# Twelve expert products grouped by PSUM bank: six into one bank, then six into the other

## The chip, the cores and the metric

The kernel runs on one core of a Trainium2 chip. The metric is the device time of one execution in microseconds (us), start to end, on that core. A core has TensorE (PE in the profile, with its weight loads as PEld), VectorE (DVE), ScalarE (ACT), GpSimd (POOL) and SyncE (SP), which here issues most of the DMAs. PE writes its results into PSUM, which has eight banks of 512 float32 columns in each of 128 partitions. The other engines read them there.

## What is computed

The reference is one layer of a hybrid model for 1024 tokens of width 1024: a norm, one projection, four mixers (sparse attention, a gated recurrent mixer, banded attention, differential attention), a gated sum, an output projection, a second norm, a router, and 32 experts. Each token goes to two experts, and the results are summed with the router's weights. The part around the change is the expert block:

```python
def expert_block(args):
    xb, e = args
    return (jax.nn.silu(xb @ w1[e]) * (xb @ w3[e])) @ w2[e]
```

`xb` are the rows of an expert's tokens (width 1024), `w1[e]` and `w3[e]` are 1024 x 512, and `w2[e]` is 512 x 1024, all float32.

## The kernel before

The layer runs in stages: `project`, `attend`, `mix`, `route`, `experts`, `combine`. The change is in `experts` (from L2101). It treats the 32 experts in order, two for each turn `i` of a loop (`j` is 0 or 1), with 96 token rows each (`CAP` = 96). There is one copy of each buffer for `j` = 0 and one for `j` = 1. Work for experts with more than 96 tokens stands behind it in `overflow`, and the change does not touch that.

A float32 product is made of three float32r products: each operand is split into a high part (a rounded copy) and a low part (what is left), and hi x hi, hi x lo and lo x hi are summed in PSUM. ScalarE makes the high part of the weights (`high_a` for w1 and w3 at L2326, `high_b` for w2 at L2335) in a ring of four buffers, `w_hi`. VectorE makes the low part in place of the weights (`low_a` at L2413, `low_b` at L2420).

The weights come in blocks of 1 MB: w1 and w3 of an expert in four (`wa`, L219; `q` = 0 to 3), w2 in two (`wd`, L223; `q` = 0, 1). SyncE issues the load of a block for the expert two further on as soon as PE has used that block (`a_used`, `b_used`).

PE's order of work for one expert is in `body`: `up` for `q` = 0 and 1, eight transposes that turn the next expert's rows (L2140), `up` for `q` = 2 and 3, `down` of the expert before, and four transposes of the hidden rows (L2146).

- `up(i, j, q)` (product at L2255) covers two blocks of K, `k` = 2q and 2q + 1, with the index `c`. The stationary operand is the transposed token block `x[:, k, :]`, 128 partitions x 96 columns. The moving operand is `w[:, c, m, :]`, 512 columns: `m` = 0 is w1, into bank 4 (`UP`), and `m` = 1 is w3, into bank 5. There are 2 x 3 x 2 = 12 products a call, 48 an expert.
- `down` (product at L2271) does the same for w2: the stationary operand is `x[:, f, :]` of the hidden rows, 128 x 96, and `h` picks one half of the 1024 output columns, into bank 6 (`Y`) or 7. There are 12 products for each of two `q`, 24 an expert.

After `up`, ScalarE takes the sigmoid of bank 4 (L2367), and VectorE multiplies (L2406, L2408). After `down`, ScalarE copies banks 6 and 7 out (L2350), and its queue stores them (L2352).

Three other stages have products of the same kind (float32r, 512 moving columns), with 128 stationary columns. L922 in `project` makes 24 products into a bank before it goes to the next. L1588, in the output projection, also makes 24. L1639, in `mix`, makes six:

```python
                for h in range(2):
                    cols = slice(h * 512, (h + 1) * 512)
                    for k in range(2):
                        ...
                        for r, (w, x) in enumerate(((w_h, y_hi[n]), (w_h, y_lo[n]), (w_l, y_hi[n]))):
                            ins = nc.tensor.matmul(psum[:, 2 * (c % 4) + h, :], w[:, k, :], x[:, k, cols],
```

In these three, too, the stationary operand is a high block twice and a low block once for each k. L2076, in `route`, is a series of small products.

Of the kernel before, what the change touches and what calls it, by code (L numbers as in the profile page):

```python
# [2100 lines left out]
def experts(nc, a, s):  # L2101
# [6 lines left out]
    wa_lo, w_hi, xg, xg_in = s.wa_lo, s.w_ring, s.xg, s.xg_in  # L2108
    wb_lo = [[sb(f"wb_lo{j}_{q}", [P, 2, DM], 128 + 16 * j + 8 * q, F32R) for q in range(2)] for j in range(2)]
    xT_hi = [sb(f"xT_hi{i}", [P, KC, CAP], 72 + 3 * i, F32R) for i in range(2)]  # L2110
    xT_lo = [sb(f"xT_lo{i}", [P, KC, CAP], 80 + 3 * i, F32R) for i in range(2)]
    hT_hi, hT_lo = sb("hT_hi", [P, FT, CAP], 78, F32R), sb("hT_lo", [P, FT, CAP], 86, F32R)
# [17 lines left out]
    def hi_a(j, q):  # L2130

        return w_hi[(6 * j + q) % 4][:, :].rearrange("p (c m n) -> p c m n", c=2, m=2)

    def hi_b(j, q):

        return w_hi[(6 * (j + 1) + 4 + q) % 4][:, :].rearrange("p (f n) -> p f n", f=2)

    def x_transposes(j):
        for c in range(KC):
            ins = nc.tensor.transpose(psum[:, c // 4, (c % 4) * CAP:(c % 4 + 1) * CAP],  # L2140
                                      xg[j][:, c * P:(c + 1) * P], s.ident[0:CAP, 0:CAP])
        return ins

    def h_transposes():
        for f in range(FT):
            ins = nc.tensor.transpose(psum[:, 2, f * CAP:(f + 1) * CAP], hid[:, f * P:(f + 1) * P],  # L2146
                                      s.ident[0:CAP, 0:CAP])
        return ins
# [16 lines left out]
    def loop(eng, body):  # L2165

        for j in range(2):
            body(0, j, j == 0, False)
        with eng.Fori(1, NE // 2 - 1) as i:
            for j in range(2):  # L2170
                body(i, j, False, False)
        for j in range(2):
            body(NE // 2 - 1, j, False, j == 1)

    def overflow(eng, body):

        blocks = eng.value_load(s.ov_i[0:1, 1, 0:1], min_val=0, max_val=N_OV)
        with eng.If(blocks > 0):
            with eng.Fori(0, N_OV) as b:
                body(b)  # L2180
# [4 lines left out]
    with nc.Block() as block:  # L2185
        @block.sync
        def _(sp):
            def refill(i, j, up, down):

                if up:  # L2190
                    for q in range(4):
                        sp.wait_ge(a_used, i * 8 + (4 * j - 8 + q + 1))
                        s.load_a(sp, i * 2 + j, j, q)
                if down:
                    for q in range(2):
                        sp.wait_ge(b_used, i * 4 + (2 * j - 6 + q + 1))
                        s.load_b(sp, i * 2 + (j - 1), 1 - j, q)

            refill(1, 0, True, False)
            refill(1, 1, True, True)  # L2200
            with sp.Fori(2, NE // 2) as i:
                for j in range(2):
                    refill(i, j, True, True)
            refill(NE // 2, 0, False, True)
            sp.wait_ge(b_used, 2 * NE)

            def body(b):
                sp.wait_ge(ov["go"], b + 1)
                e = expert_of(sp, b)
                for q in range(4):  # L2210
                    s.load_a(sp, e, 0, q, ov["weights"])
                for q in range(2):
                    s.load_b(sp, e, 0, q, ov["weights"])
            overflow(sp, body)
# [31 lines left out]
        @block.tensor  # L2246
        def _(pe):
            def up(i, j, q):

                pe.wait_ge(a_low, i * 8 + (4 * j + q + 1))  # L2250
                for c in range(2):
                    k = 2 * q + c
                    for x, w in ((xT_hi[j], hi_a(j, q)), (xT_hi[j], wa_lo[j][q]), (xT_lo[j], hi_a(j, q))):
                        for m in range(2):
                            ins = nc.tensor.matmul(psum[0:CAP, UP + m, :], x[:, k, :], w[:, c, m, :],  # L2255
                                                   start=(k == 0 and x is xT_hi[j] and w is not wa_lo[j][q]),
                                                   stop=(k == KC - 1 and x is xT_lo[j]))
                ins.then_inc(a_used, 1)

            def down(i, j, first):  # L2260

                pe.wait_ge(hT_low, i * 2 + (j + 1))
                if not first:
                    pe.wait_ge(y_taken, i * 2 + j)
                for q in range(2):
                    pe.wait_ge(b_low, i * 4 + (2 * j + q + 1))
                    for c in range(2):
                        f = 2 * q + c
                        for x, w in ((hT_hi, hi_b(j, q)), (hT_hi, wb_lo[j][q]), (hT_lo, hi_b(j, q))):
                            for h in range(2):  # L2270
                                ins = nc.tensor.matmul(psum[0:CAP, Y + h, :], x[:, f, :],  # L2271
                                                       w[:, c, h * 512:(h + 1) * 512],
                                                       start=(f == 0 and x is hT_hi and w is not wb_lo[j][q]),
                                                       stop=(f == FT - 1 and x is hT_lo))
                    ins.then_inc(b_used, 1)

            def body(i, j, start, last):
                if start:
                    pe.wait_ge(xg_in[0], 16)
                    x_transposes(0).then_inc(xT_ready, 1)  # L2280
                pe.wait_ge(xT_low, i * 2 + (j + 1))
                up(i, j, 0)
                up(i, j, 1)
                if not last:
                    pe.wait_ge(xg_in[1 - j], i * 16 + (16 + 16 * j))
                    x_transposes(1 - j).then_inc(xT_ready, 1)
                up(i, j, 2)
                up(i, j, 3)
                if not start:
                    down(i if j else i - 1, 1 - j, isinstance(i, int) and i * 2 + j == 1)  # L2290
                pe.wait_ge(hid_ready, i * 2 + (j + 1))
                h_transposes().then_inc(hT_ready, 1)
            loop(pe, body)
            down(NE // 2 - 1, 1, False)
            pe.wait_ge(y_taken, NE)

            def body(b):
                pe.wait_ge(ov["rows"], b * 16 + 16)
                x_transposes(0).then_inc(ov["xT"], 1)
                pe.wait_ge(ov["xT_taken"], b + 1)  # L2300
                pe.wait_ge(ov["weights"], b * 96 + 96)
                for k in range(KC):
                    for m in range(2):
                        ins = nc.tensor.matmul(psum[0:CAP, UP + m, :], xT_ov[:, k, :], wa[0][k // 2][:, k % 2, m, :],
                                               start=(k == 0), stop=(k == KC - 1))
                ins.then_inc(ov["up"], 1)
                pe.wait_ge(ov["hid"], b + 1)
                h_transposes().then_inc(ov["hT"], 1)
                pe.wait_ge(ov["hT_taken"], b + 1)
                for f in range(FT):  # L2310
                    for h in range(2):
                        ins = nc.tensor.matmul(psum[0:CAP, Y + h, :], hT_ov[:, f, :],
                                               wb[0][f // 2][:, f % 2, h * 512:(h + 1) * 512],
                                               start=(f == 0), stop=(f == FT - 1))
                ins.then_inc(ov["y"], 1)
            overflow(pe, body)
# [270 lines left out]
```

## Time and profile before

| | |
|---|---|
| Time, median of 3 runs | 1860.6 us (1859.17 to 1860.83) |
| Span of the profiled execution, first to last instruction | 1856.9 us |
| What lies around the span, against the median | 3.7 us |
| Mean granted TensorE clock over the span | 0.967 |
| PE busy | 1738.5 us (94%) |
| VectorE busy | 1457.9 us (79%) |
| ScalarE busy | 941.4 us (51%) |
| Expert products (L2255 and L2271), first and last start | 1230.4 and 1806.9 us |

How to read it: busy time is the time in which an engine has an instruction under way, and PE's products overlap each other, so that a product's duration is longer than the distance to the next start. The granted clock is TensorE's clock as a share of its full 2.4 GHz.

### The profile page before, as it was taken

To read this page: it belongs to the slowest core of one execution; us is meant where nothing else is said; L and a number is where in the kernel's file an instruction comes from. 1 tells how busy PE (TensorE), PEld (TensorE's weight loads), DVE (VectorE), ACT (ScalarE), POOL (GpSimd) and SP (SyncE) were. 2 spreads that over 40 slices of the span, in tenths; PEclk is the share of its full clock that TensorE was granted. 3 is DMA by queue.
4 is the path that set the end of the run, shared out by engine and by line. 5 is a ranking of instruction groups with operands and counts; after the bars stand their busy time and mean duration, and the time that the engine had idled before them with its cause. 6 is when DMAs were issued, how large, how long until landed. Compare 5 with 4: busy or idle time off the path is not lost. (4 is left out here: it accounts for less than half of the span.)

```text
span 1856.9 us, 24076 instructions
## 1 busy us (share of the span) xinstructions
PE 1738.5 (94%) x8726; PEld 1315.4 (71%) x8726; DVE 1457.9 (79%) x2108; ACT 941.4 (51%) x1207; POOL 151.7 (8%) x129
## 2 busy tenths in 40 slices
PE   7999999999999999999999989859999999999980
PEld 7768877777777777777767767747777777777750
DVE  5587869989788878766629965679999999999956
ACT  6533121133434445545556520147777877878752
POOL 1100000000000000000000000002212122122003
PEclk9999999999999999999999989869999999999995
DMA  5202222112443322313206820299999999999937
GB/s 198 68 11 82 84 75 69 57 57 74 164 136 118 109 65 66 136 54 108 80 35 253 312 83 35 94 339 374 393 398 405 396 395 404 392 400 404 404 116 285
DMA packets 75920, 358.76 MB, mean 193 GB/s; under 512 B 8636, under 2 KB 11228, under 8 KB 49340
## 3 DMA queue, kind: packets, MB, share of 16 engines
q1 hardware_dynamic: 66364, 324.08, 46.6%
q0 software_dynamic: 5888, 20.97, 3.4%
q10 hardware_dynamic: 3584, 12.58, 1.7%
q8 instruction: 52, 0.85, 0.2%
q14 instruction: 32, 0.26, 0.0%
HBM read 301.63 MB, written 55.98 MB: 193 GB/s over the span
## 5 line engine op out<-in xcount | busy, mean ns | idle before, releaser
L2413 DVE TENSOR_TENSOR wa_lo<-wa,w_hi 128x2048 fp32r<-128x2048 f32 x127 | 287.6, 2286 | 15.5 <-ACT w_hi L2326 14.1
L2326 ACT ACTIVATE w_hi<-wa 128x2048 fp32r<-128x2048 f32 x127 | 242.8, 1915 | 63.0 <-PE psum L2271 36.4
L1470 PE MATMUL psum<-h_hi,w_hi 128*128 128x512 f32 x512 | 213.2, 416 | 4.0 <-DVE w_lo L153 2.1
L1470 PE MATMUL psum<-h_hi,w_lo 128*128 128x512 f32 x512 | 205.5, 401 | 0.0
L1470 PE MATMUL psum<-h_lo,w_hi 128*128 128x512 f32 x512 | 203.0, 396 | 0.0
L167 DVE MAX8 top<-sel 128x8 f32<-128x384 f32 (+5 forms) x192 | 171.3, 892 | 4.8
L2420 DVE TENSOR_TENSOR wb_lo<-wd,w_hi 128x2048 fp32r<-128x2048 f32 x64 | 143.9, 2288 | 34.7 <-ACT w_hi L2335 34.7
L165 DVE MATCH_REPLACE8 sel<-top,sel 128x384 f32<-128x384 f32 (+5 forms) x192 | 168.1, 875 | 0.0
L2255 PE MATMUL psum<-w_hi,xT_hi 128*96 128x512 f32 x512 | 164.8, 403 | 1.9 <-DVE xT_lo L2428 1.9
L2255 PE MATMUL psum<-w_hi,xT_lo 128*96 128x512 f32 x512 | 160.6, 394 | 0.0
L2255 PE MATMUL psum<-wa_lo,xT_hi 128*96 128x512 f32 x512 | 160.5, 395 | 0.0
L1470 PEld LDWEIGHTS psum<-h_hi,w_hi 128*128 128x128 f32 x512 | 96.9, 189 | 46.4 <-issue 18.9
L2335 ACT ACTIVATE w_hi<-wd 128x2048 fp32r<-128x2048 f32 x64 | 122.4, 1914 | 3.8 <-PE psum L2255 2.3
L1197 ACT ACTIVATE pt<-psum 128x512 f32<-128x512 f32 (+3 forms) x144 | 61.3, 471 | 118.9 <-PE psum L1490 118.7
L922 PE MATMUL psum<-h_hi,w_hi 128*128 128x512 f32 x288 | 117.5, 408 | 0.0
L1470 PEld LDWEIGHTS psum<-h_hi,w_lo 128*128 128x128 f32 x512 | 96.6, 189 | 25.5 <-issue 5.1
L922 PE MATMUL psum<-h_hi,w_lo 128*128 128x512 f32 x288 | 112.6, 391 | 0.0
L922 PE MATMUL psum<-h_lo,w_hi 128*128 128x512 f32 x288 | 112.3, 390 | 0.0
L1470 PEld LDWEIGHTS psum<-h_lo,w_hi 128*128 128x128 f32 x512 | 97.1, 190 | 19.6 <-issue 2.7
L2255 PEld LDWEIGHTS psum<-wa_lo,xT_hi 128*96 128x96 f32 x512 | 83.1, 162 | 36.1
L2255 PEld LDWEIGHTS psum<-w_hi,xT_lo 128*96 128x96 f32 x512 | 83.1, 162 | 35.9
L2255 PEld LDWEIGHTS psum<-w_hi,xT_hi 128*96 128x96 f32 x512 | 78.7, 164 | 29.6 <-DVE xT_lo L2428 2.2
(378 smaller groups left out, 3387.6 us busy)
## 6 DMA issues: line engine op xcount, KB each, us to landing
wa<-expert_up SPq DMA_DIRECT2D x128, 1024.0 KB, 11.0
wd<-expert_down SPq DMA_DIRECT2D x64, 1024.0 KB, 11.1
w<-w_gate SPq DMA_DIRECT2D x32, 512.0 KB, 4.1
gate_pre<-gate_out SPq DMA_DIRECT2D x64, 256.0 KB, 3.2
gate<-gate_pre SPq DMA_DIRECT2D x32, 512.0 KB, 6.1
ys<-yo ACTq DMA_DIRECT2D x32, 384.0 KB, 6.9
w<-w_T SPq DMA_DIRECT2D x18, 512.0 KB, 3.8
ys<-zeros SPq DMA_DIRECT2D x7, 1152.0 KB, 5.9
```

The source lines that it names most:

```text
L165: link(nc.vector.match_replace(sc, top8[:, :], sc, TAKEN))
L167: link(nc.vector.max(top8[:, :], sc))
L922: ins = nc.tensor.matmul(psum[:, bank + h, :], w[:, k, :], x[:, k, h * 512:(h + 1) * 512], start=(k == 0 and r == 0), stop=(k == KC - 1 an ...
L1197: nc.scalar.activation(dst, src, ACT.Copy).then_inc(pt_copied, 1)
L1470: ins = nc.tensor.matmul(psum[:, 7, :], w[:, k, :], x[:, k, half * 512:(half + 1) * 512], start=(n == 0), stop=(n == BURST - 1))
L2255: ins = nc.tensor.matmul(psum[0:CAP, UP + m, :], x[:, k, :], w[:, c, m, :], start=(k == 0 and x is xT_hi[j] and w is not wa_lo[j][q]), sto ...
L2326: nc.scalar.activation(hi_a(j, q).rearrange("p c m n -> p (c m n)"), wa[j][q][:, :, :, :].rearrange("p c m n -> p (c m n)"), ACT.Copy).the ...
L2335: nc.scalar.activation(hi_b(j, q).rearrange("p f n -> p (f n)"), wb[j][q][:, :, :].rearrange("p f n -> p (f n)"), ACT.Copy).then_inc(b_hig ...
L2413: nc.vector.tensor_tensor(wa_lo[j][q][:, :, :, :].rearrange("p c m n -> p (c m n)"), wa[j][q][:, :, :, :].rearrange("p c m n -> p (c m n)" ...
L2420: nc.vector.tensor_tensor(wb_lo[j][q][:, :, :].rearrange("p f n -> p (f n)"), wb[j][q][:, :, :].rearrange("p f n -> p (f n)"), hi_b(j, q). ...
```

## The change

In `up`, the loop over `m` (the bank) moves from inside to outside. Before, each product goes to the other bank than the one before it; after, the six products of both `c` and the three terms go to bank 4, then the same six to bank 5. In `down`, the loop over `h` moves in the same way, inside each `q`. Waits, semaphore counts and operands are the same, and the last product of each twelve is the same one.

```diff
@@ up
-                for c in range(2):
-                    k = 2 * q + c
-                    for x, w in ((xT_hi[j], hi_a(j, q)), (xT_hi[j], wa_lo[j][q]), (xT_lo[j], hi_a(j, q))):
-                        for m in range(2):
+                for m in range(2):
+                    for c in range(2):
+                        k = 2 * q + c
+                        for x, w in ((xT_hi[j], hi_a(j, q)), (xT_hi[j], wa_lo[j][q]), (xT_lo[j], hi_a(j, q))):
                             ins = nc.tensor.matmul(psum[0:CAP, UP + m, :], x[:, k, :], w[:, c, m, :],
                                                    start=(k == 0 and x is xT_hi[j] and w is not wa_lo[j][q]),
                                                    stop=(k == KC - 1 and x is xT_lo[j]))
@@ down
-                    for c in range(2):
-                        f = 2 * q + c
-                        for x, w in ((hT_hi, hi_b(j, q)), (hT_hi, wb_lo[j][q]), (hT_lo, hi_b(j, q))):
-                            for h in range(2):
+                    for h in range(2):
+                        for c in range(2):
+                            f = 2 * q + c
+                            for x, w in ((hT_hi, hi_b(j, q)), (hT_hi, wb_lo[j][q]), (hT_lo, hi_b(j, q))):
                                 ins = nc.tensor.matmul(psum[0:CAP, Y + h, :], x[:, f, :],
                                                        w[:, c, h * 512:(h + 1) * 512],
```

## Rows read from the trace of the kernel before

**Rows 1.** The page's slices: busy tenths of 40 equal slices of the span.
```profile
PE   7999999999999999999999989859999999999980
DMA  5202222112443322313206820299999999999937
```

**Rows 2.** Stretches: us; busy (count) of PE, PEld, DVE, ACT, POOL; clock; DMA share; GB/s.
```profile
1300.00:1400.00 100.00, 100.00 (x481) 71.36 (x479) 90.91 (x57) 79.36 (x58) 21.18 (x12) 1.00 1.01 398
...
1600.00:1700.00 100.00, 100.00 (x481) 71.36 (x479) 90.98 (x57) 79.38 (x58) 21.71 (x12) 1.00 1.01 400
```

**Rows 3.** Who waited for whom, 1300 to 1780 us: us, times, longest.
```profile
ACT w_hi L2326 <- PE psum L2271: 34.0, 56, 0.9
```

**Rows 4.** Timeline of one expert: start us, length of the merged row, instructions.
```profile
1512.64 0.50 PE L2146 MATMUL psum<-ident,hid 96*128 96x96 f32 x4
1512.92 0.68 PE L2255 MATMUL psum<-w_hi,xT_hi 128*96 128x512 f32 x2
1513.44 0.62 PE L2255 MATMUL psum<-wa_lo,xT_hi 128*96 128x512 f32 x2
...
1518.06 0.62 PE L2255 MATMUL psum<-w_hi,xT_lo 128*96 128x512 f32 x2
1518.52 0.82 PE L2140 MATMUL psum<-ident,xg 96*128 96x96 f32 x8
1519.12 0.68 PE L2255 MATMUL psum<-w_hi,xT_hi 128*96 128x512 f32 x2
...
1530.26 0.50 PE L2146 MATMUL psum<-ident,hid 96*128 96x96 f32 x4
```

**Rows 5.** Timeline of L922, L1639 and L1588: first and last of a row of products.
```profile
159.97 0.39 PE L922 MATMUL psum<-h_hi,w_lo 128*128 128x512 f32 x1
...
178.33 0.39 PE L922 MATMUL psum<-h_hi,w_lo 128*128 128x512 f32 x1
...
1001.01 0.39 PE L1639 MATMUL psum<-y_hiB,wb_hi 128*128 128x512 f32 x1
...
1010.30 0.39 PE L1639 MATMUL psum<-y_hiA,wb_lo 128*128 128x512 f32 x1
...
1119.92 0.40 PE L1588 MATMUL psum<-w_out_lo,mix_hi 128*128 128x512 f32 x1
...
1120.39 0.40 PE L1588 MATMUL psum<-w_out_hi,mix_hi 128*128 128x512 f32 x1
...
1122.01 0.39 PE L1588 MATMUL psum<-w_out_lo,mix_hi 128*128 128x512 f32 x1
```

**Rows 6.** L2255, all of it: duration ns min/median/max, first and last start.
```profile
L2255 PEld LDWEIGHTS psum<-w_hi,xT_lo x512: 160/161/277, 1231.8 to 1787.9; 128*96 128x96 f32 x171
L2255 PE MATMUL psum<-w_hi,xT_lo x512: 387/392/628, 1232.2 to 1788.1; 128*96 128x512 f32 x171
```

**Rows 7.** The same of L922 and of the twelves of one expert, durations in ns.
```profile
L922 PE MATMUL psum<-h_hi,w_hi x27: 389/389/389, 160.2 to 177.9; 128*128 128x512 f32 x27
...
L2255 PE MATMUL psum<-wa_lo,xT_hi x4: 389/392/395, 1513.4 to 1515.1; 128*96 128x512 f32 x4
...
L2255 PE MATMUL psum<-wa_lo,xT_hi x4: 392/392/397, 1516.2 to 1517.8; 128*96 128x512 f32 x4
...
L2271 PE MATMUL psum<-wb_lo,hT_hi x4: 389/392/395, 1525.2 to 1526.8; 128*96 128x512 f32 x4
...
L2271 PE MATMUL psum<-wb_lo,hT_hi x4: 392/392/397, 1528.0 to 1529.6; 128*96 128x512 f32 x4
```

**Rows 8.** Loads of wa: landing in us at 1300 to 1360 and 1660 to 1720; timeline.
```profile
DMA to landing us min/median/max: 9.4/10.0/10.7
...
DMA to landing us min/median/max: 12.4/12.8/13.9
...
1516.09 9.29 SPq L219 DMA_DIRECT2D wa<-expert_up  x4
...
1539.77 1.92 ACT L2326 ACTIVATE w_hi<-wa 128x2048 fp32r<-128x2048 f32 x1 [0.82 <-PE psum L2255]
```

## The prediction

> **What bounds the kernel now.** The slices of the span come first [rows 1]: TensorE (PE) is at nine tenths nearly everywhere, and in the last third of the span, where the experts run, so are the DMA engines. The table by stretches [rows 2] says which of the two sets the pace there. From 1300 to 1700 us PE is busy 100.00 of every 100 us at a granted clock of 1.00, VectorE 91 and ScalarE 79. The DMA share reads 1.01 and the rate about 399 GB/s. So PE never pauses, and DMA has nothing to spare either. The table of waits agrees: it names neither a wait of PE nor one for a DMA, and ScalarE's longest in total is one for PE [rows 3]. Hence the time of the experts is the sum of the distances between the starts of PE's products.
>
> The timeline of one expert [rows 4] gives these. From 1512.64 to 1530.26 us one expert takes 17.62 us. From 1513.44 to 1518.06 us twenty products start, 4.62 us, so one product takes 0.2310 us. The 72 products of an expert (48 up, 24 down) are then 16.63 us. The rest is the twelve transposes (0.28 and 0.60 us up to the next product) and a first product in each of two runs that is about 0.06 us longer. Busy times are of no use here: a product shows 0.39 us [rows 6] and overlaps the next, so only starts count.
>
> Is 0.2310 us the best that PE does? In two other stages it does a little better. L922 starts 81 products from 159.97 to 178.33 us, 0.2267 us each, and L1639 41 from 1001.01 to 1010.30 us, 0.2266 us each [rows 5]. Both keep to a bank for several products. The difference of 0.0042 us is the only thing in the trace that the change could win, and it could win it only if changing the bank is its cause.
>
> **The change part by part.** No product, weight load, transpose, wait, semaphore or DMA is added or removed. In each of the 192 groups of twelve (6 an expert, 32 experts), the same twelve products are reordered, and the twelfth is the same product as before, so what ScalarE, VectorE and SyncE wait for comes at the same count. Nothing is moved past another queue. Three things differ:
>
> - Bank changes. Before, each product goes to the other bank: 12 changes a group. After, one in the middle and one at the next group: 2. That takes away 10 × 192 = 1920 changes. The nearest row for one change is L1639: it goes to another bank every six products (its loop over h has two products of K for each of three terms), which makes about 7 changes among those 41 starts, and it still runs at 0.2266 us, where L922, which changes bank only after 24 products, runs at 0.2267. All seven together cost less than the 0.01 us that the timeline resolves, under 0.002 us each. Product sum of the likeliest case: 0.
> - The stationary operand. Before, four products in a row load the same hi block and then two the same lo block; after, two and one. No load is skipped before (512 loads in each row of L2255, one for each product [rows 6]), so none is lost. Two hi and one lo is also the pattern of L922 and L1639, both at 0.2267 us. Cost 0.
> - Which k follows which. Within a group the two k now alternate, two visits each in place of one.
>
> Why are the experts slower, if not by banks? They differ from L922 in more than the bank: their stationary block has 96 columns, not 128. The durations within one expert hint at this [rows 7]. They are modelled, but they follow the distance to the next start. In L922 each is 389 ns, 81 times over. In the experts they differ, and the pattern goes with the position among four k: the products with a low block of weights show 389/392/395 in the first twelve of a 24 and 392/392/397 in the second. That is so in up and in down, although down follows up without a pause and up follows transposes. A bank pattern would repeat every two products, and a semaphore pattern every twelve. What repeats after four k is the place of a 96-column block in its tile. The reordering leaves those blocks where they are. This is an inference, no measurement; it is why I take 0.2310 us for after as well.
>
> Bounds for the unknown. Best: all 2304 products at L922's rate, 2304 × 0.0042 = 9.7 us less. Worst near row: after small products, L1588 starts nine products from 1119.92 to 1122.01 us, 0.2322 us each [rows 5]. If the more frequent change of k kept the experts in that state, it is 2304 × 0.0012 = 2.8 us more. The only mechanism for a larger loss is the second rival below.
>
> Sum: 1856.9 us of span, plus 0. The median of the runs shown, 1860.6, lies 3.7 us over the span of the profiled execution; a change of the sum is carried to it as it is. So 1860.6.
>
> The Trainium skill has a rule by which the change would pay: TensorE: Matmul & The Clock Gate, "A second HAM failure mode: psum-queue depth-cycling", tells of a kernel whose cycling through banks let PE pause between groups often enough that its clock fell and rose. By that, fewer bank changes would give clock back. Here the granted clock is already 1.00 throughout [rows 2], 2.4 GHz, so it gives nothing back, and the sum by that rule is again 1860.6; no run here shows a kernel in which it bites.
>
> **The rivals.**
>
> *Bank changes are the 0.0042 us.* Then the experts come to L922's rate, though not at once: L1588 shows nine slower distances in a row after small products [rows 5], so I take ten for each run, and an expert has two unbroken runs (48 and 24), which leaves 20 of 72 slow. 52 × 32 × 0.0042 = 7.0 us: 1853.6, and at best 1850.9. For it: the long one-bank streams are at 0.2267, and the only stage that alternates is at 0.2310. Against it: L1639's single changes are free, and L1588 shows the slow rate in one bank too, so alternating is not needed for it. DMA would not take this gain away, though it is nearly the bound. A load takes a median of 10.0 us to land at 1300 to 1360 us and 12.8 at 1660 to 1720 [rows 8]. That is 2.8 us in 360, or 0.14 us more for each expert of 17.62, so DMA needs about 17.62 + 0.14 = 17.76 us an expert. With PE at 17.40 the delay would grow by 0.36 each, some 10 us until the last load. The load issued at 1516.09 us lands some 11.3 us later if the delay grows evenly between those two stretches, and ScalarE takes it at 1539.77 [rows 8], 12.4 us later still. It just fits. A gain of twice the size would run dry, a reason why the low end stops where it does.
>
> *The same bank again costs.* With one bank, each product adds to what the product right before it wrote, where now there is a product between. With 128 columns that costs nothing (L922). With 96 columns no row has it. If it put the experts at the 0.235 us that the first two distances of L1588 show (1119.92 to 1120.39 us [rows 5]), the price is 0.004 × 2304 = 9.2 us: 1869.8. It decides from 0.0016 us a product on (3.7 us in all).
>
> *The reordering matters, but only by the k that alternate.* Up to the 2.8 us above, on the slow side: 1863.4, which counts as no change.
>
> **How the numbers follow.** A measurement of this kernel tells about 0.2% (3.7 us) from no change. No effect, the forecast: 0.66. Banks as the cause, a gain of 7.0 to 9.7 us: 0.25, and with it the faster side by over 0.2%. The k that alternate, within 0.2%: 0.04. The same bank costs: 0.05, slower. So faster 0.25, same 0.70, slower 0.05. The predicted time is 1860.6. The likeliest case's own range is 1858.8 to 1862.2 (twice the scatter of the runs). The full range reaches just past the first rival's own value, to 1853.0, and to the bound of the third, 1863.5; left out are the slow rival and the better part of the first one's span, about 0.15 together.
>
> **What would show it.** In the timeline of an expert in the changed kernel the rows come in the order of one bank's six products, and ten pairs or more of starts should still give 0.2310 us a product and 17.62 us an expert. PE stays at 100.00 in each stretch, and a landing time that creeps up to 12.8 us in the end says that the pace is the same. If bank changes were the cause, the products would start 0.2267 us apart after the first ten of a run, the durations would all be 389, the expert would take 17.40 us and landings would reach 18 us or so. If the same bank costs, the starts are 0.233 us or more apart and landings fall. What would make the prediction wrong is most of all that a bank change costs only if it comes at every product, which no row tests.

## The result

The changed kernel takes 1861.92 us, the kernel before 1858.80 us (medians of 16 runs each, run in turn). The ratio is 1.0016, with a 95% interval from 1.0009 to 1.0023: it is 0.16% slower, or some 3 us. That lies inside the predicted range and within the 0.2% that the prediction called no change, but it is clear of zero, and the forecast was zero.

The stretches of the experts and the slices look as before [rows 1, 2]. PE never pauses, and DMA is full:

```profile
1300.00:1400.00 100.00, 100.00 (x477) 71.05 (x476) 90.50 (x57) 79.14 (x57) 21.76 (x12) 1.00 1.01 400
...
1600.00:1700.00 100.00, 100.00 (x479) 71.14 (x478) 90.50 (x57) 79.55 (x57) 21.75 (x12) 1.00 1.02 400
```

With PE at 100.00 in both kernels, these rows can't show that its products are further apart. The starts in the timeline show it. These are one expert of the changed kernel (answering to [rows 4]):

```profile
1511.62 0.49 PE L2146 MATMUL psum<-ident,hid 96*128 96x96 f32 x4
1511.90 0.45 PE L2255 MATMUL psum<-w_hi,xT_hi 128*96 128x512 f32 x1
1512.18 0.39 PE L2255 MATMUL psum<-wa_lo,xT_hi 128*96 128x512 f32 x1
1512.41 0.40 PE L2255 MATMUL psum<-w_hi,xT_lo 128*96 128x512 f32 x1
1512.65 0.39 PE L2255 MATMUL psum<-w_hi,xT_hi 128*96 128x512 f32 x1
...
1517.52 0.82 PE L2140 MATMUL psum<-ident,xg 96*128 96x96 f32 x8
```

The order is the new one: hi, low weights, low tokens, then the other k. The best measure is from one expert's hidden transposes to the same ones many experts later. The first two rows are of the kernel before, 21 experts apart:

```profile
1301.20 0.49 PE L2146 MATMUL psum<-ident,hid 96*128 96x96 f32 x4
...
1671.22 0.49 PE L2146 MATMUL psum<-ident,hid 96*128 96x96 f32 x4
```

And these are of the changed kernel, 20 apart:

```profile
1317.07 0.49 PE L2146 MATMUL psum<-ident,hid 96*128 96x96 f32 x4
...
1670.80 0.49 PE L2146 MATMUL psum<-ident,hid 96*128 96x96 f32 x4
```

Before, 370.02 / 21 = 17.620 us an expert; after, 353.73 / 20 = 17.687. Divided by 72 products, the 0.067 us are 0.9 ns a product. Over all 2304 products that is 2.1 us, most of the 3 us. The durations changed as well: the median of the products with the low token block was 392 ns [rows 6] and is 395.

```profile
L2255 PE MATMUL psum<-w_hi,xT_hi x368: 389/394/450, 1299.7 to 1699.9; 128*96 128x512 f32 x184
L2255 PE MATMUL psum<-wa_lo,xT_hi x367: 387/392/398, 1299.9 to 1699.5; 128*96 128x512 f32 x184
L2255 PE MATMUL psum<-w_hi,xT_lo x367: 392/395/400, 1300.2 to 1699.7; 128*96 128x512 f32 x184
```

The loads show no relief for DMA. The delay of a load is 8.8 us at 1300 to 1360 and 11.8 at 1660 to 1720, against 10.0 and 12.8 [rows 8]. It grows by 3.0 us, before by 2.8, and the lower level at the start is no sign of the slower PE: e2 below, at the pace of the kernel before, has 8.7 there. A larger step does show: e10, at 17.787 us an expert, goes from 9.4 to 9.7.

```profile
DMA to landing us min/median/max: 8.2/8.8/9.6
...
DMA to landing us min/median/max: 11.1/11.8/13.1
```

The two profiled executions have the same span, 1856.9 us. That is chance. The changed one reached its experts' first product 1.9 us earlier (1228.5 us, before 1230.4), lost 2.1 us from the first to the last hidden transpose (1244.7 to 1794.2 us, before 1246.7 to 1794.1), and lost another 0.5 us in the last `down`, which starts at a granted clock of 0.50 after PE's last wait. What follows its last product was 0.5 us shorter (49.2 us, before 49.7). Part of the last `down`'s 0.5 us is luck too, as shown below.

### The profile page after: what moved, and what is told of

It reads as the page before. It is cut to its first block and busy times, and to the rows that moved or that the text cites. A ratio compares the mean times of both kernels' runs of the same rounds, so it can differ in the third digit from the quotient of the medians.

```text
span 1856.9 us, 24076 instructions
## 1 busy us (share of the span) xinstructions
PE 1738.6 (94%) x8726; PEld 1313.9 (71%) x8726; DVE 1458.3 (79%) x2108; ACT 941.7 (51%) x1207; POOL 150.6 (8%) x129
## 5 line engine op out<-in xcount | busy, mean ns | idle before, releaser
L2255 PE MATMUL psum<-w_hi,xT_hi 128*96 128x512 f32 x512 | 206.5, 403 | 1.9 <-DVE xT_lo L2428 1.9
L2255 PE MATMUL psum<-w_hi,xT_lo 128*96 128x512 f32 x512 | 203.2, 397 | 0.0
L2255 PE MATMUL psum<-wa_lo,xT_hi 128*96 128x512 f32 x512 | 202.0, 394 | 0.0
L922 PE MATMUL psum<-h_hi,w_hi 128*128 128x512 f32 x288 | 117.5, 408 | 0.0
L922 PE MATMUL psum<-h_hi,w_lo 128*128 128x512 f32 x288 | 112.6, 391 | 0.0
L922 PE MATMUL psum<-h_lo,w_hi 128*128 128x512 f32 x288 | 112.3, 390 | 0.0
L2255 PEld LDWEIGHTS psum<-w_hi,xT_lo 128*96 128x96 f32 x512 | 82.9, 162 | 36.3
L2271 PE MATMUL psum<-w_hi,hT_hi 128*96 128x512 f32 x256 | 101.9, 398 | 5.9 <-DVE wb_lo L2420 5.9
L2255 PEld LDWEIGHTS psum<-w_hi,xT_hi 128*96 128x96 f32 x512 | 83.2, 163 | 33.6 <-DVE xT_lo L2428 2.2
```

The lines of the kernel that those rows point to most:

```text
L922: ins = nc.tensor.matmul(psum[:, bank + h, :], w[:, k, :], x[:, k, h * 512:(h + 1) * 512], start=(k == 0 and r == 0), stop=(k == KC - 1 an ...
L2271: ins = nc.tensor.matmul(psum[0:CAP, Y + h, :], x[:, f, :], w[:, c, h * 512:(h + 1) * 512], start=(f == 0 and x is hT_hi and w is not wb_l ...
```

## Experiments

Each is the kernel before with the edit shown. `ORDER` is the order of the twelve products of a group as (c, term, bank), where c picks the k, and term 0, 1, 2 are hi x hi, hi x low weights, low tokens x hi. The place of a product is where its stationary block starts, which differs between an even and an odd k; "3, 3, 3, 3" means three products at one place, three at the other, and so on. The pitch is the distance from the start of one block to the start of the next, 384 bytes where nothing else is said. Us an expert come from two rows of hidden transposes as above; ns a product are what this is over 17.620, divided by 72. The kernels e2, e4, e7, e9, e11, f6, f3 and f2 compute other sums than the reference and serve to measure the pace alone.

| run | sequence of places, twelve products | us an expert | ns a product against before | ratio of times (95% interval) |
|---|---|---|---|---|
| before | 6 at one k, 6 at the other | 17.620 | 0 | 1 |
| changed kernel | 3, 3, 3, 3 | 17.687 | +0.9 | 1.0016 (1.0009 to 1.0023) |
| e1 | 3, 3, 3, 3; banks alternate | 17.686 | +0.9 | 1.0018 (1.0007 to 1.0029) |
| e2 | 6, 6; one bank a group | 17.620 | 0 | 0.9997 (0.9988 to 1.0007) |
| e3 | 6, 6; c, bank, term | 17.620 | 0 | 0.9994 (0.9985 to 1.0004) |
| e4 | the first block always | 17.560 | -0.8 | 0.9990 (0.9980 to 0.9999) |
| e5 | 6, 6; pitch 512 bytes | 17.560 | -0.8 | 0.9999 (0.9990 to 1.0009) |
| e6 | 6, 6; pitch 512, 128 columns | 17.473 | -2.0 | 0.9973 (0.9963 to 0.9983) |
| e7 | 3, 3, 3, 3; pitch 256 bytes | 17.560 | -0.8 | none; one run, 1855.43 us |
| e8 | 3, 3, 3, 3; pitch 512 bytes | 17.560 | -0.8 | 1.0005 (0.9995 to 1.0014) |
| e9 | the second block always | 17.680 | +0.8 | none; one run, 1858.40 us |
| e10 | 1, 1, 1, ... | 17.787 | +2.3 | 1.0038 (1.0022 to 1.0054) |
| e11 | 3, 3, 3, 3; 128 columns, pitch 384 | 17.727 | +1.5 | none; one run, 1861.73 us |
| f6 | 6, 6; from the high tile alone | 17.620 | 0 | none; one run, 1859.80 us |
| f3 | 3, 3, 3, 3; from the high tile alone | 17.687 | +0.9 | none; one run, 1863.06 us |
| f2 | 2, 2, 2, 2, 2, 2; from the high tile alone | 17.673 | +0.7 | none; one run, 1861.49 us |

**Is it the bank or the order of the operands?** e1 keeps the new order of the operands and changes the bank each time; e2 keeps the old order and stays in a bank for twelve.

```diff
+ORDER = [(c, r, (c + r + s) % 2) for s in range(2) for c in range(2) for r in range(3)]   # e1
+psum[0:CAP, UP + q % 2, :] ... psum[0:CAP, Y + q, :]                                      # e2
```

> The twelve products of a group take the stationary and moving blocks in the order of the changed kernel as far as k and the three terms go (hi, hi, lo of one k, then of the other, and all of it again), but the bank changes at each product, as before. Operands theory (the slowdown of 1.0 ns a product comes from the order of the operands): distance of starts in the experts 0.2318 us, span and time as the changed kernel, some 2 to 3 us over the kernel before. Bank theory (two products in a row into the same bank cost): 0.2309 us, time as before.

> Operands in the order of the kernel before, but all twelve products of a group go to one bank (bank 4 or 5, 6 or 7, by q), so that the bank changes once in twelve; the sums in the banks are not those of the reference. Operands theory: 0.2309 us a product, time as before. Bank theory: 0.2318 us or more, 2 to 3 us slower or more. The rival of the prediction (bank changes are the 0.0042 us): 0.2267 us after ten products, 7 us faster.

e1's rows, 21 experts apart, give the changed kernel's pace:

```profile
1304.77 0.49 PE L2147 MATMUL psum<-ident,hid 96*128 96x96 f32 x4
...
1676.18 0.49 PE L2147 MATMUL psum<-ident,hid 96*128 96x96 f32 x4
```

e2's give the pace of the kernel before to the last digit, 370.02 us for 21:

```profile
1299.78 0.49 PE L2147 MATMUL psum<-ident,hid 96*128 96x96 f32 x4
...
1669.80 0.49 PE L2147 MATMUL psum<-ident,hid 96*128 96x96 f32 x4
```

So the bank plays no part in the pace, in either direction. The bank theory and the prediction's first two rivals fall; the whole slowdown of the pace comes with the order of the operands.

**Which part of the order?** e3 changes the stationary and moving blocks as often as the changed kernel (eight times in twelve), but finishes one k before the other. e4 has the changed kernel's order with one stationary block for all.

```diff
+ORDER = [(c, r, m) for c in range(2) for m in range(2) for r in range(3)]   # e3
...
-x[:, k, :]
+xT_hi[j][:, 0, :]                                                           # e4, and hT_hi[:, 0, :]
```

> Order c outside, then the bank, then the three terms: one k is finished for both banks before the other starts, as in the kernel before, but the stationary block changes eight times in twelve products in place of four, and the bank four times. If what costs is each change of a stationary or moving block: 0.2318 us a product. If what costs is that the two k alternate: 0.2309 us. Bank theory: between the two, nearer to 0.2318.

> Order of the changed kernel, but every product of the experts takes the same stationary block (the high part of the first k), so the sums are not those of the reference; weight loads are still issued for each product. If changes of the stationary block cost the 1.0 ns: 0.2309 us a product or less. If the moving blocks' order or the bank costs it: 0.2318 us. If the place of a 96-column block in its tile makes the experts slower than other stages: 0.2267 us.

e3 is at the old pace, 17.620 us, and e4 below it:

```profile
1303.37 0.50 PE L2147 MATMUL psum<-ident,hid 96*128 96x96 f32 x4
...
1672.13 0.49 PE L2147 MATMUL psum<-ident,hid 96*128 96x96 f32 x4
```

These are 21 experts, 368.76 / 21 = 17.560 us each. It is not the number of changes of block, nor the moving operand. What counts is which k the stationary block belongs to, that is, where in the tile it starts. But the place is not all that holds the experts back from L922's 0.2267 us. In e4, thirteen distances from 1303.93 to 1306.92 us come to 0.2300 us each:

```profile
1303.93 0.39 PE L2255 MATMUL psum<-wa_lo,xT_hi 128*96 128x512 f32 x1
...
1306.92 0.39 PE L2255 MATMUL psum<-w_hi,xT_hi 128*96 128x512 f32 x1
```

**Is it the address?** A block of 96 float32 columns is 384 bytes, one and a half times 256. So every second k starts 128 bytes off a multiple of 256. e5 and e8 give the tiles a pitch of 128 columns (with the hidden tiles moved to free room) and still load 96; e7 reads 96 columns at steps of 64 columns (256 bytes) in the old tiles.

```diff
-xT_hi = [sb(f"xT_hi{i}", [P, KC, CAP], 72 + 3 * i, F32R) for i in range(2)]
+xT_hi = [sb(f"xT_hi{i}", [P, KC, P], 72 + 4 * i, F32R) for i in range(2)]
...
-x[:, k, :]
+x[:, k, 0:CAP]                                              # e5 old order, e8 new order
+x[:, :, :].rearrange("p k n -> p (k n)")[:, 64 * k:64 * k + CAP]   # e7, new order
```

> The transposed token and hidden blocks get a pitch of 128 columns (512 bytes) in their tiles in place of 96 (384 bytes), and the products still load 96 of them; order of the kernel before. Place theory (each step to a block whose address differs in its low bits adds some 5.3 ns, twice in twelve products before): 0.2300 us a product as with one block, 2304 x 0.0009 = 2 us faster than before. If the step to another k costs whatever its address: 0.2309 us, time as before.

> Order of the changed kernel, the products read their 96 columns at steps of 64 columns (256 bytes) in the unchanged tiles, so the sums are not those of the reference. If only the address within 256 bytes matters: 0.2300 us a product. If the address within 512 bytes matters, or each change of k: 0.2318 us.

> Pitch of 128 columns, 96 loaded, order of the changed kernel. Place theory: 0.2300 us a product, 2 us faster than the kernel before, and the change costs nothing any more. If the step to another k costs whatever its address: 0.2318 us, 2 to 3 us slower than before.

All three are at 17.560 us an expert. e8 has the changed kernel's order and pays nothing for it in pace:

```profile
1301.34 0.49 PE L2147 MATMUL psum<-ident,hid 96*128 96x96 f32 x4
...
1670.10 0.49 PE L2147 MATMUL psum<-ident,hid 96*128 96x96 f32 x4
```

The address within 256 bytes is what matters to the pace; of the possible offsets, 0 and 128 bytes were measured. The time gained did not show as it should: 2304 x 0.8 ns = 1.9 us is 0.9990, which e5's interval just reaches and e8's does not. The profile of e8 names one place where time was given back in that execution. Its last `down` starts at 1798.79 us and its last product at 1806.57, 7.78 us; before, it is from 1800.34 to 1807.16, 6.82 us (the 1806.9 us of the table of before is the last row of the timeline, and a second product of that row starts at 1807.16). The stretches around it, first of the kernel before, then of e8, show why (us; busy time and count of PE; granted clock; DMA share; GB/s):

```profile
1797.00:1800.00 3.00, 0.00 (x0) 0.50 0.09 33
1800.00:1804.00 4.00, 3.66 (x10) 0.57 0.00 0
1804.00:1808.00 4.00, 3.56 (x16) 1.00 0.00 0
```

```profile
1797.00:1800.00 3.00, 1.21 (x3) 0.54 0.00 0
1800.00:1804.00 4.00, 4.00 (x11) 0.50 0.00 0
1804.00:1808.00 4.00, 2.96 (x13) 0.99 0.00 0
```

In both, PE waited 5.95 us before that `down` and went on at half clock (0.50 is 1.2 GHz); in e8 more of its products fell into the slow piece. e5's profile shows the same, 7.81 us. Over the sixteen traces the last `down` takes 6.80 us (e2) to 7.81 us (e5), and it is the longer the more of it stands at 0.50; the kernel before, with e2 and e3, is at the low end. So its profile had luck there. Up to the last hidden transposes e5 did gain what its pace says: 545.57 us from the first one, before 547.42. Whether the timed runs of e5 and e8 lost their gain in the last `down` is not shown.

**A price for each step?** After e4 to e8 I held that each step between a k on and a k off the multiple costs 5.3 ns. e9 and e10 test this from both ends.

```diff
+xT_hi[j][:, 1, :]                                                            # e9, order as e4
+ORDER = [(c, r, m) for r in range(3) for m in range(2) for c in range(2)]   # e10
```

> As the run with one stationary block, but the block is the second one of the tile, 384 bytes on (128 bytes past a multiple of 256), so the sums are not those of the reference. If each step between places that differ within 256 bytes costs, and not the place itself: 0.2300 us a product as with the first block. If a block that starts off a multiple of 256 bytes is slower to load: more than 0.2300 us, 0.2318 or so.

> The two k alternate at each product (order: term, bank, k), twelve steps in a group in place of two before and four in the changed kernel. If each step costs 5.3 ns: 0.2300 + 0.0053 = 0.2353 us a product, 2304 x 0.0044 = 10 us slower than before. If what costs is a stay at a place of less than some length, or if the loads adapt: less than that.

The theory of a price for each step falls. e9 has no step at all and is slow:

```profile
1316.53 0.49 PE L2147 MATMUL psum<-ident,hid 96*128 96x96 f32 x4
...
1670.13 0.49 PE L2147 MATMUL psum<-ident,hid 96*128 96x96 f32 x4
```

353.60 / 20 = 17.680 us, 1.7 ns a product more than with the first block. Starting off the multiple costs by itself. The record of the weight load doesn't show where: it is as long in e9 (the second row) as in e4 (the first).

```profile
L2255 PEld LDWEIGHTS psum<-w_hi,xT_hi x732: 160/162/164, 1303.6 to 1699.9; 128*96 128x96 f32 x183
...
L2255 PEld LDWEIGHTS psum<-w_hi,xT_hi x733: 161/162/163, 1300.1 to 1699.5; 128*96 128x96 f32 x184
```

Half the products of the kernel before start off the multiple: half of 1.7 ns over e4 is 0.8 ns, and that is the kernel before. The changed kernel has just as many of them and costs 0.9 ns more, so the switching comes on top. At e10's switch for every product it is 2.3 ns, about half of what was expected:

```profile
1303.99 0.49 PE L2147 MATMUL psum<-ident,hid 96*128 96x96 f32 x4
...
1677.51 0.49 PE L2147 MATMUL psum<-ident,hid 96*128 96x96 f32 x4
```

**The places alone.** The f runs take the stationary operand from the high tile only, at the first or second block by the number n of the product in its group, with banks and moving operands as before.

```diff
+xT_hi[j][:, (n // 6) % 2, :]     # f6; f3 has n // 3, f2 has n // 2
```

> All products take the stationary operand from the high tile alone, the first or the second block, six of one and six of the other in twelve (the steps of the kernel before); moving operands and banks in the order before; the sums are not those of the reference. If only the place counts and not the tile (hi or lo): 0.2309 us a product as before.

> The same with three of one and three of the other in turn (the steps of the changed kernel). If the steps between places alone make the 1.0 ns of the changed kernel: 0.2318 us. If it takes the step from lo to hi at the same time: 0.2309 us.

> The same with two and two. A cost for each step of some 2.5 ns over the half-and-half 0.2308 us: 0.2308 + 6/12 x 0.0025 = 0.2320 us. If the cost saturates from runs of three on: 0.2318 us.

f6 (the first two rows) takes 370.02 us for 21 experts, the kernel before; f3 (the last two) 371.42, the changed kernel:

```profile
1301.93 0.49 PE L2147 MATMUL psum<-ident,hid 96*128 96x96 f32 x4
...
1671.95 0.49 PE L2147 MATMUL psum<-ident,hid 96*128 96x96 f32 x4
...
1303.14 0.49 PE L2147 MATMUL psum<-ident,hid 96*128 96x96 f32 x4
...
1674.56 0.49 PE L2147 MATMUL psum<-ident,hid 96*128 96x96 f32 x4
```

The sequence of places alone makes the difference. It is not a smooth law: stays of six cost 0, of three 0.9, of two 0.7, of one 2.3 ns a product over the kernel before. In f2 the experts alternate between 17.664 and 17.682 us, and 0.7 is their mean; why they alternate is open.

**What keeps the experts from 0.2267 us?** e6 has the old order, with a bank change at each product, on tiles with a pitch of 128 columns, and loads all 128. The last 32 columns are filled once, and their results in PSUM are not read.

```diff
+nc.scalar.activation(x[:, :, CAP:P], s.ident[:, 0:P - CAP].unsqueeze(1).to_broadcast([P, nk, P - CAP]), ACT.Copy)
...
-nc.tensor.matmul(psum[0:CAP, UP + m, :], x[:, k, :], ...
+nc.tensor.matmul(psum[:, UP + m, :], x[:, k, :], ...
...
+x[:, :, :].rearrange("p k n -> p (k n)")[:, CAP * (k if k < 7 else 5):][:, 0:P]   # e11, old tiles, new order
```

> Pitch of 128 columns, and the products load all 128 (the last 32 are filled once and their rows of PSUM are never read); order of the kernel before, banks alternating at each product. If the 96 columns are what keeps the experts from the rate of L922: 0.2267 us a product after some ten, and 2304 x 0.0042 = 7 to 9.7 us faster than before. If something else of the experts' stage (DMA load, waits, four equal blocks in a row) keeps them slow: 0.2300 us, 2 us faster.

> Order of the changed kernel and the tiles unchanged (384 bytes a block), but each product loads 128 columns from its place, over the end of the block; the last block is replaced by an earlier one that lies the same within 256 bytes, so part of the sums is not that of the reference. If the step costs with any number of columns: 0.2267 + 0.0018 = 0.2285 us in the steady part. If it costs only with 96 columns: 0.2267 us.

```profile
1307.68 0.62 PE L2257 MATMUL psum<-w_hi,xT_lo 128*128 128x512 f32 x2
...
1315.84 0.62 PE L2273 MATMUL psum<-w_hi,hT_lo 128*128 128x512 f32 x2
1316.30 0.41 PE L2148 MATMUL psum<-ident,hid 96*128 96x96 f32 x3
```

From 1307.68 to 1315.84 us there are 36 distances, 0.2267 us each: L922's rate, in the experts, with DMA full and the bank changing every time. So 96 columns against 128 were the rest of the difference (the product then also writes 128 partitions of PSUM in place of 96; the two were not separated). The time is 0.9973 of before, 5 us less, and e6 is the fastest of all, 1854.24 us. The delay of its loads grows as the first rival reckoned, from 10.6 us at 1300 to 17.7 at 1660, and still the waits from 1300 to 1780 us name no load:

```profile
DMA to landing us min/median/max: 9.8/10.6/11.9
...
DMA to landing us min/median/max: 17.0/17.7/18.3
```

e11 loads 128 columns from the old places, in the changed kernel's order. At 17.727 us an expert it is 0.25 us over e6, 3.5 ns a product, about twice the 1.8 that was expected; 96 columns in that order lie 0.13 us over the aligned ones (17.687 against 17.560). Off the multiple, the wider load is hurt more than the narrow one. In this order the 128 columns pay only on aligned blocks; in the order of the kernel before, no run has them on the old places.

## Why the prediction was right or wrong

- **What bounds the stage** was right. The time of the experts is the sum of the distances between PE's starts. Every run that moved the distance moved the stretch from the first to the last hidden transposes by it; the last `down` adds its own scatter, up to 1 us.
- **Bank changes at 0** was right, to the resolution of the trace (e1, e2). L1639 had been the right row to read.
- **Stationary changes at 0** was right for changes between the high and the low block (e3, f3).
- **"Which k follows which" is the step that failed.** It stood in the list of what differs and got no price. The next paragraph then inferred that the place of a 96-column block in its tile makes the pattern of durations, and concluded that "The reordering leaves those blocks where they are." That they stay is true, but the products visit them in another sequence: stays of three in place of six. That sequence alone costs 0.9 ns a product (f3), 2.1 us in all.
- **The third rival named the right cause, and its size is luck.** It put up to 2.8 us on the alternating k. The measured difference of the medians is 3.1 us, of which the products' distances explain 2.1. But its 1.2 ns a product came from L1588's slow start after small products. That is another matter: e6, with all its blocks aligned, starts slow after its transposes too (nine distances of 231 ns in the mean). And alternating costs nothing where the blocks are aligned (e7, e8). It got a chance of 0.04 and should have been the forecast, since the prediction itself held the place of the block to be what makes the experts slow.
- **The repeat after four k** was misread. f6 uses two places only, over and over, and its products with the low weights still show the durations of [rows 7], one set in the first twelve of an expert and the other in the second. So what repeats after four k is not the place. That the place matters turned out true, but these durations were no evidence for it; what makes the longer pattern is open. The two rows of f6:

```profile
L2255 PE MATMUL psum<-wa_lo,xT_hi x4: 389/392/395, 1514.2 to 1515.8; 128*96 128x512 f32 x4
...
L2255 PE MATMUL psum<-wa_lo,xT_hi x4: 392/392/397, 1516.9 to 1518.6; 128*96 128x512 f32 x4
```

- **The first rival's sum** (a gain of 7.0 us at L922's rate, DMA just keeping up) was right as arithmetic: e6 gained 0.147 us an expert on the old pace, 4.7 us, while its loads grew late by about 7 us, but by columns and pitch, not by banks. The first ten products of each run stay slow as reckoned, and the first product after transposes costs a little more (0.31 us to the next start, before 0.29), so it is less than 7.0.
- **The second rival** (the same bank costs) has nothing to it (e2). The changed kernel's 0.9 ns a product is under the 1.6 ns that it asked for.
- About 1 us of the 3 is not placed. The interval of the ratio reaches from 1.7 to 4.3 us, so the 2.1 us of the distances would do by themselves, and the last `down` moves by up to 1 us with the piece at half clock (e8 against before).

The rule of the Trainium skill that the prediction weighed (TensorE: Matmul & The Clock Gate, "A second HAM failure mode: psum-queue depth-cycling") did nothing here: e2, which changes the bank once in twelve products in place of each time, keeps the pace and the time of the kernel before, and in the traces of all sixteen kernels the granted clock is 1.00 from 1260 to 1787 us, whatever the banks.

## What to carry to other kernels

When PE is the bound, measure from start to start over many products; busy time and durations hide a per cent. Where the same products run at two rates in two stages, list all that differs in the operands (columns, pitch, order of addresses), not only what the change is about. Give the stationary blocks of float32r products a pitch of a multiple of 256 bytes, and try the full 128 columns even if the last 32 are of no use: here the two together were worth 0.27%. The pitch alone quickened the experts' pace by 0.3%, but no gain in the time was measured (e5, e8), and regrouping the banks was worth nothing.

## What the runs showed of the hardware

- A stationary float32r block of 96 columns that starts 128 bytes off a multiple of 256 adds 1.7 ns to each product (e9 against e4), though the record of the load is no longer for it (162 ns in both) and ends some 66 ns before the next product starts.
- Switching between aligned and unaligned blocks adds more, up to 2.3 ns a product over the half-and-half of the kernel before (e10), and not in step with the number of switches (f2 costs less than f3).
- With aligned blocks, products of 96 stationary columns start 0.2300 us apart, those of 128 columns 0.2267 us (e4, e6): fewer columns are slower, although their load is shorter (161 ns [rows 6], 188 ns in e6). Why is not shown.
- Changing the PSUM bank at each product, or never in twelve, made a difference of 0.00 us in 370 (e2 against before).
